# Decode heads turned back by transposes, the own key's value added on VectorE, and the two heads of a pair in turn

## What is computed

```python
h = rmsnorm(x, g_mix); proj = h @ w_in                 # pool channels | q | k | v, 512 columns each
x = x + concat(pool_mix(u), moba_attend(q, k, v)) @ w_out   # 8 heads of 64; decode: 256 cached keys + its own
x = x + cross_attend(rmsnorm(x, g_cross), mk, mv)      # 4 heads of 256, 256 memory keys for each sequence
x = x + square(relu(rmsnorm(x, g_mlp) @ w_up)) @ w_down
y = rmsnorm(x, g_final)
```

## Time and profile before

| | us |
|---|---|
| median of 3 runs | 451.04 |
| the three runs | 448.37, 451.04, 451.50 |
| profiled execution, first to last instruction (span) | 447.9 |
| TensorE busy | 423.8 |
| VectorE busy | 266.7 |
| ScalarE busy | 229.5 |
| GpSimd busy | 39.1 |

### The profile page before, as it was taken

The page is one execution under the profiler, slowest core; times in us unless marked ns, Lnnn a source line. Parts: engine busy times, 40 slices in busy tenths (PEclk is TensorE's granted clock), DMA queues, the critical chain, the costliest instruction groups (busy, mean ns, idle before and its releaser), DMA issues.

```text
span 447.9 us, 8424 instructions
## 1 busy us (share of the span) xinstructions
PE 423.8 (95%) x3346; PEld 393.0 (88%) x3346; DVE 266.7 (60%) x417; ACT 229.5 (51%) x411; POOL 39.1 (9%) x49
## 2 busy tenths in 40 slices
PE   2699899999999999999999999999999999999992
PEld 2699787787988999795599999999999999999992
DVE  2676787889454587654316967766666633444304
ACT  5777657664355474434026746656666533353202
POOL 0621001450000030000002200000000000020000
PEclk9979999999999999999989999999999999999998
DMA  7899897485699887597716655555555555545002
GB/s 273 286 280 343 324 265 240 161 283 170 185 352 317 334 277 284 173 368 281 266 36 246 235 190 187 189 190 189 187 187 184 186 180 176 176 168 179 1 1 97
DMA packets 42409, 96.80 MB, mean 216 GB/s; under 512 B 3954, under 2 KB 20466, under 8 KB 42234
## 3 DMA queue, kind: packets, MB, share of 16 engines
q1 hardware_dynamic: 40962, 93.03, 60.9%
q10 hardware_dynamic: 1408, 3.23, 1.9%
HBM read 91.94 MB, written 4.54 MB: 215 GB/s over the span
## 4 chain that ended last, share of the span: by engine, by line
PE 77%; ACT 8%; DVE 7%; issue 3%; DMA 2%; POOL 2%; ACTq 0%; SPq 0%; DVEq 0%; POOLq 0%
PE psum L865 68%; PE psum L666 4%; ACT w_hi L881 2%; DVE w_lo L1080 2%; DMA raw<-in_w_in 2%; POOL ssq L1306 1%; ACT swapped L881 1%; PE psum L791 1%; PE psum L778 1%; ACT soft L1024 1%; ACT act_hi L881 1%; DVE soft L1191 1%; PE psum L813 1%; DVE stats L1194 1%; PE psum L686 0%
## 5 line engine op out<-in xcount | busy, mean ns | idle before, releaser
L1080 DVE TENSOR_TENSOR w_lo<-raw,w_hi 128x1024 fp32r<-128x1024 f32 x82 | 103.1, 1268 | 90.5 <-ACT w_hi L881 90.0
L865 PE MATMUL psum<-act_hi,w_hi 128*128 128x264 f32 (+1 forms) x416 | 122.5, 294 | 9.0 <-DVE act_lo L1084 8.0
L881 ACT ACTIVATE w_hi<-raw 128x1024 fp32r<-128x1024 f32 x82 | 85.5, 1054 | 76.3 <-PE psum L865 64.2
L865 PE MATMUL psum<-act_lo,w_hi 128*128 128x264 f32 (+1 forms) x416 | 119.7, 288 | 0.0
L865 PE MATMUL psum<-act_hi,w_lo 128*128 128x264 f32 (+1 forms) x416 | 119.5, 287 | 0.0
L865 PEld LDWEIGHTS psum<-act_hi,w_hi 128*128 128x128 f32 x416 | 80.2, 193 | 12.9 <-DVE w_lo L1080 8.3
L865 PEld LDWEIGHTS psum<-act_lo,w_hi 128*128 128x128 f32 x416 | 80.0, 192 | 0.2
L865 PEld LDWEIGHTS psum<-act_hi,w_lo 128*128 128x128 f32 x416 | 79.8, 192 | 0.0
L1306 POOL TENSOR_TENSOR ssq<-ssq,sq 128x264 f32<-128x264 f32 (+1 forms) x31 | 25.4, 818 | 339.5 <-ACT sq L902 337.0
L865 PE MATMUL psum<-hid_hi,w_hi 128*128 128x264 f32 x176 | 50.1, 284 | 0.0
L865 PE MATMUL psum<-hid_lo,w_hi 128*128 128x264 f32 x176 | 50.1, 284 | 0.0
(11 more groups left out here) (155 smaller groups left out, 769.1 us busy)
## 6 DMA issues: line engine op xcount, KB each, us to landing
raw<-in_w_down SPq DMA_DIRECT2D x20, 512.0 KB, 3.3
raw<-in_w_up SPq DMA_DIRECT2D x18, 512.0 KB, 4.3
raw<-in_w_in SPq DMA_DIRECT2D x16, 512.0 KB, 5.4
raw_more<-in_w_up SPq DMA_DIRECT2D x14, 512.0 KB, 4.4
raw_more<-in_w_down SPq DMA_DIRECT2D x12, 512.0 KB, 4.2
keysT<-in_cache_k SPq DMA_DIRECT2D x16, 256.0 KB, 4.4
stage<-in_cache_v SPq DMA_DIRECT2D x16, 256.0 KB, 4.1
raw<-in_w_ck SPq DMA_DIRECT2D x8, 512.0 KB, 5.2
```

Source lines behind the costliest of these rows:

```text
L865: mm = pe.matmul(out, a, b, start=first and m == 0, stop=end_ and m == 2)
L881: return nc.scalar.activation(out, in_, ACT.Copy, scale=scale)
L1080: V.tensor_tensor(lo_of(c), raw_of(c), hi_of(c).bitcast(F32), ALU.subtract).then_inc(w_lo_ready, 1)
```

## The change

Five things are changed.

- `c_attn` and `xc_attn` transpose `opart` in full, 128x128 four times, and the copies out of PSUM pick each head's element with strides (`own_heads`). With that the tables `diag_q`, `diag_x`, `rowsel` and `own` go, and VectorE's pass into `opart` becomes a plain copy for `xc_O`.
- `xc_attn` is one job for each batch and half, four in all; the copies are in two parts for each (two rows of ScalarE and two of VectorE).
- The own key's weight is taken straight from the softmax (`ownp`, one column for each batch), and VectorE adds weight times `vown` to the result of `cO` as it writes `opart`. The product of line 743 and the one of line 737 go, and with the latter the wait for `t_copied`.
- `vown` holds the own value of each sample in its 32 rows. GpSimd loads it: once the three stores of `v_nat` have landed in HBM (`v_stored`), it issues 8 transfers that read back `v_sample`, one row each, spread over 32 partitions. They stand ahead of `add_squares("m")`.
- `S` and `O` issue the products of the two heads of a pair in turn; `S(2i)` and `S(2i+1)` both wait for their banks first.

```diff
-        ("xc_O", 1, 0), ("xc_attn", 0), ("xc_O", 1, 1), ("xc_attn", 1))
+        ("xc_O", 1, 0), ("xc_attn", 0, 0), ("xc_attn", 0, 1), ("xc_O", 1, 1), ("xc_attn", 1, 0), ("xc_attn", 1, 1))
...
+OPART_END = {("cO", b): ("c_attn", b) for b in range(2)} | {("xc_O", b, h): ("xc_attn", b, h) for b in range(2) for h in range(2)}
...
-        sb("beside_projections", [P, (3 * AT + 8) * T - KT * MEM - 2 * D], F32, mixers)
+        vown = sb("vown", [P, 2, AW], F32, mixers)
+        sb("beside_projections", [P, (3 * AT + 8) * T - KT * MEM - 2 * D - 2 * AW], F32, mixers)
         v_nat = sb("v_nat", [P, 3, AW], F32, mixers)
-        ownp = sb("ownp", [DEC, P], F32, mixers)
+        ownp = sb("ownp", [P, 2], F32, mixers)
...
+        def own_heads(job, part):
+
+            what, b, *half = job
+            t0 = SEQ + 4 * b
+            B = psum[:, PLACE[job][0], :]
+            out = []
+            for e in range(2):
+                if what == "c_attn":
+                    rows, k = slice(e * HD, (e + 1) * HD), slice(AT, KT)
+                    src = bass.AP(tensor=B.tensor, offset=B.offset + e * HD * 8 * CN + e, ap=[[8 * CN, HD], [P + 2, AT], [32, 4]])
+                else:
+                    rows, k = slice(0, P), slice(AT * half[0] + 2 * e, AT * half[0] + 2 * e + 2)
+                    src = bass.AP(tensor=B.tensor, offset=B.offset + 2 * e * P + 2 * half[0] + e, ap=[[8 * CN, P], [P, 2], [32, 4]])
+                out.append((part[rows, k, t0:t0 + 4], src, mix_hi[rows, k, t0:t0 + 4]))
+            return out
...
                 elif what == "S":
                     h = i[0]
+                    if h % 2:
+                        return
                     if h == 0:
                         pe.wait_ge(rope_done, 2 * AT)
-                    r, f = HD * (h % 2), h // 2
-                    q, k = qT[r:r + HD, f, :], kT[r:r + HD, f, :]
-                    pe.matmul(B[:, 0:P], q[:, 0:P], k[:, 0:P], start=True, stop=True)
-                    last = pe.matmul(B[:, P:3 * P], q[:, P:2 * P], k[:, 0:SEQ], start=True, stop=True)
+                    begin(("S", h + 1))
+                    pair = [(bank_of(("S", h + e)), qT[HD * e:HD * e + HD, h // 2, :], kT[HD * e:HD * e + HD, h // 2, :]) for e in range(2)]
+                    for S, q, k in pair:
+                        pe.matmul(S[:, 0:P], q[:, 0:P], k[:, 0:P], start=True, stop=True)
+                    for e, (S, q, k) in enumerate(pair):
+                        end(("S", h + e), pe.matmul(S[:, P:3 * P], q[:, P:2 * P], k[:, 0:SEQ], start=True, stop=True))
+                    return
...
                 elif what == "O":
                     for e in range(2):
-                        h = 2 * i[0] + e
-                        t = SOFT_T["P_T", h]
-                        wait_out(pe, ("P_T", h))
-                        if h == 0:
-                            for tt in range(3):
-                                wait_out(pe, ("v_nat", tt))
-                        o, pT = B[HD * e:HD * e + HD, :], softT[:, t % SOFT_TS, :]
-                        pe.matmul(o[:, 0:SEQ], v_nat[:, 0, h * HD:(h + 1) * HD], pT[:, 0:SEQ], start=True, stop=False, skip_group_check=True)
-                        last = pe.matmul(o[:, P:SEQ], v_nat[:, 1, h * HD:(h + 1) * HD], pT[:, SEQ:3 * P], start=False, stop=True, skip_group_check=True)
+                        wait_out(pe, ("P_T", 2 * i[0] + e))
+                    if i[0] == 0:
+                        for tt in range(3):
+                            wait_out(pe, ("v_nat", tt))
+                    for c in range(2):
+                        for e in range(2):
+                            h = 2 * i[0] + e
+                            o, pT = B[HD * e:HD * e + HD, :], softT[:, SOFT_T["P_T", h] % SOFT_TS, :]
+                            last = pe.matmul(o[:, c * P:SEQ], v_nat[:, c, h * HD:(h + 1) * HD], pT[:, c * SEQ:(c + 2) * P if c == 0 else 3 * P], start=c == 0, stop=c == 1, skip_group_check=True)
...
                     for c in range(2):
-                        pe.transpose(B[:, c * P:(c + 1) * P], p[:, c * P:(c + 1) * P], ident)
-
-                    last = pe.matmul(B[0:DEC, PAST:PAST + P], p[:, PAST:PAST + 1].broadcast_to([P, DEC]), ident, start=True, stop=True)
+                        last = pe.transpose(B[:, c * P:(c + 1) * P], p[:, c * P:(c + 1) * P], ident)
                 elif what == "cO":
                     b = i[0]
                     wait_out(pe, ("cP_T", b))
                     pT = softT[:, SOFT_T["cP_T", b] % SOFT_TS, :]
 
-                    pe.matmul(B, ownp[:, :], v_nat[0:DEC, 2, :], start=True, stop=False, skip_group_check=True)
                     for c in range(2):
                         for j in range(4):
                             if c == 0:
                                 landed(pe, ("V", 4 * b + j))
-                            last = tile4(B[32 * j:32 * j + 32, :], pT[:, c * P + 32 * j:c * P + 32 * j + 32], chunked(("V", 4 * b + j))[:, c, :], j, False, c == 1)
-                elif what == "c_attn":
-                    b = i[0]
-                    wait_out(pe, ("cO", b))
+                            last = tile4(B[32 * j:32 * j + 32, :], pT[:, c * P + 32 * j:c * P + 32 * j + 32], chunked(("V", 4 * b + j))[:, c, :], j, c == 0, c == 1)
+                elif what in ("c_attn", "xc_attn"):
+                    of = ("cO" if what == "c_attn" else "xc_O", *i)
+                    wait_out(pe, of)
                     for f in range(AT):
-                        last = pe.matmul(B[:, 4 * f:4 * f + 4], opart[:, OPART["cO", b] % 2, f * P:(f + 1) * P], con("rowsel"), start=True, stop=True)
+                        last = pe.transpose(B[:, f * P:(f + 1) * P], opart[:, OPART[of] % 2, f * P:(f + 1) * P], ident)
...
-                elif what == "xc_attn":
-                    b = i[0]
-                    for half in range(2):
-                        wait_out(pe, ("xc_O", b, half))
-                        for f in range(AT):
-                            last = pe.matmul(B[:, 4 * (AT * half + f):4 * (AT * half + f) + 4], opart[:, OPART["xc_O", b, half] % 2, f * P:(f + 1) * P], con("rowsel"), start=True, stop=True)
...
+                    copy(softT[:, n % SOFT_TS, 0:size], B[:, 0:size]).then_inc(free, 1)
+                elif what in ("c_attn", "xc_attn"):
+                    wait_full(act, job)
+                    for _, src, high in own_heads(job, mix_hi):
+                        last = copy(high, src)
+                    last.then_inc(hi_ready, 1)
...
-                parts = {"S": [(0, P), (P, 3 * P)], "cS": [(0, NKEY)]}.get(what, [(0, MEM), (MEM, 2 * MEM)])
+                if what == "cS":
+                    V.tensor_scalar(ownp[:, i[0]:i[0] + 1], soft[:, slot, PAST:NKEY], stats[:, slot, 4:5], None, ALU.mult).then_inc(own_weight_ready, 1)
+                parts = {"S": [(0, P), (P, 3 * P)], "cS": [(0, PAST)]}.get(what, [(0, MEM), (MEM, 2 * MEM)])
...
-                elif what == "cP_T":
-                    b = i[0]
-                    dve.wait_ge(t_copied, b + 1)
-                    if b:
-                        wait_full(dve, ("cO", b - 1))
-                    V.tensor_tensor(ownp[:, :], B[0:DEC, PAST:PAST + P], con("own", DEC)[:, b * P:(b + 1) * P], ALU.mult).then_inc(free, 1)
                 elif what in ("cO", "xc_O"):
                     wait_full(dve, job)
                     prior = before(OPART, job, 2)
                     if prior:
                         wait_full(dve, OPART_END[prior])
-                    diag = con("diag_q") if what == "cO" else con("diag_x")[:, 2 * i[1]:2 * i[1] + 2]
-                    heads = diag.shape[1]
-                    V.tensor_tensor(opart[:, OPART[job] % 2, :].rearrange("p (h n) -> p h n", h=heads), B.rearrange("p (h n) -> p h n", h=heads),
-                                    diag.unsqueeze(2).broadcast_to([P, heads, CN // heads]), ALU.mult).then_inc(free, 1)
-                elif what in ("O", "xP_O", "c_attn", "xc_attn", "pool"):
+                    if what == "cO":
+                        dve.wait_ge(vown_landed, 16 * DEC)
+                        dve.wait_ge(own_weight_ready, i[0] + 1)
+                        V.scalar_tensor_tensor(out=opart[:, OPART[job] % 2, :], in0=vown[:, i[0], :], scalar=ownp[:, i[0]:i[0] + 1], in1=B, op0=ALU.mult, op1=ALU.add).then_inc(free, 1)
+                    else:
+                        V.tensor_copy(opart[:, OPART[job] % 2, :], B).then_inc(free, 1)
+                elif what in ("c_attn", "xc_attn"):
+                    dve.wait_ge(hi_ready, HI[job] + 1)
+                    for dst, src, high in own_heads(job, mix_lo):
+                        last = V.tensor_tensor(dst, src, high.bitcast(F32), ALU.subtract)
+                    last.then_inc(free, 1)
...
+            gp.wait_ge(v_stored, 48)
+            gp.wait_ge(rope_done, 2 * AT)
+            v_rows = outs["v_sample"].rearrange("l b a h d -> (l b a) (h d)")
+            for s in range(DEC):
```

(18 more changed lines are left out.)

6 lines of the change are left out of this document (2 added, 4 removed).

## The result

| | median us | runs |
|---|---|---|
| kernel before | 449.83 | 17 |
| changed kernel | 446.27 | 17 |

The ratio is 0.9908, with a 95% interval of 0.9889 to 0.9927: the change makes the kernel 0.9% faster. Timed again beside other kernels it was 0.9933 (0.9906 to 0.9960). The profiled span went from 447.9 to 444.5, by 3.4 us.

What follows compares the result with a forecast made beforehand. TensorE, busy 95%, was taken as the bound, except about 47 to 102 us, where ScalarE and VectorE were. +3.3 - 1.43 - 0.3 = +1.6 us, span 449.5; with 3.1 carried over, 452.6; range 448.3 to 455.0.

Steps and rivals of the forecast that it cites:

- the issue time c: Time GpSimd needs to issue one of its eight transfers; taken as 1.0 us, with 0.53 as lower bound.
- the +3.3 at 102.47: Late transfers and a clock fall make TensorE ready only at 105.8, so work after VectorE's `mkT` comes 3.3 us later.
- The formula: Delay of ScalarE's square of tile 4: 73.3 + 8c + 0.78 - 79.09 us; 3.0 us at c = 1.0.
- A: Rival: the transfers fit in, c 0.63 or less, nothing late; -1.7 us, 449.3; chance 0.32.
- the decode products: `cO(1)` at 106.19 and `c_attn(1)`, in TensorE's stretch: dropped product -1.05, transposes -0.38, together -1.43 us.
- the tail: End of cross attention: the second `xc_attn`'s cheaper transposes gain 0.3 us, between 0 and 0.65.
- The terms hidden before 102.47: Savings in `cO(0)`, line 737 and `c_attn(0)`, 2.0 us: none reaches the end while VectorE's chain stands.
- D: Rival: the shorter tail keeps TensorE's clock at the end of cross attention, 1.6 us more gained, 447.7; chance 0.07.
- B: The forecast case: c from 0.75 to 1.2, transfers late; 450.6 to 454.2, likeliest 452.6; chance 0.42.
- C: Rival: GpSimd and VectorE hold each other up; with c = 1.5, `ck` 6.7 us late, 456.6; chance 0.14.
- The pairs' order: `S` and `O` issuing a pair's two heads in turn: taken as 0, bounded by 0.3 us either way.
- The wait for `vown`: In `cO(0)`: loads land before VectorE's reader; a wait there would tie VectorE to GpSimd and refute the prediction.

Runs made afterwards that it cites:

- 16 issues: Changed kernel with GpSimd's 8 transfers as 16 of half a row each, the same bytes: 450.53 us, ratio 1.0009.
- The padded table: Kernel before, table of cross attention's folds padded with zero columns from 4 to 64: 449.26 us, ratio 1.0000; run again 448.02, ratio 0.9984.
- the sums later: Changed kernel, GpSimd's first three additions ahead of its transfers and its pooling sums waiting until VectorE split 22 chunks: 446.07 us, ratio 0.9911.

## Why the prediction was wrong

**The step that failed is the issue time c.** The prediction had ScalarE's 0.53 as the lower bound and took 1.0, by the ratio of the engines' additions. Measured: 0.51 an issue, in both kernels, with 64 and with 32 KB. The nearest row, an issue on another engine, was right; the ratio came from arithmetic on 128x256 elements and said nothing about issuing. So the delay of 3.0 us at the square was 0.08, and the +3.3 at 102.47 did not come. The Trainium skill, "DMA: Bandwidth & Descriptors", section "Latency and other measured facts", gives about 1 us to the first byte of a software-generated transfer. No run here shows a first byte; 2.9 to 5.8 us passed from issue to landing, and the engine was held for 0.51.

The formula stood: 74.20 + 4.10 + 0.78 - 79.09 is 0.0. But its start of 73.3 was 0.9 early (74.20; 72.57 to 75.49 in all eight profiles with the loads), and with 74.20 the bound below which nothing is late is c = 0.51 instead of 0.63. The transfers fitted in with nothing to spare. With 16 issues the formula gives 72.57 + 8.11 + 0.78 = 81.46, and the square stood at 81.54; `ck` came 2.6 later than before and the work at 102.47 3.7, where the forecast for 3.0 us of delay had 2.7 and 3.3.

**A and its sum.** With c right, A is what remains: -1.43 for the decode products, -0.3 for the tail. Measured -1.50 and -0.20 between the first two profiles; 1.4 for the first stands in seven of eight profiles, the second is within their spread. The terms hidden before 102.47 stayed hidden: TensorE's wait grew from 0.57 to 1.88. The 0.36 gained at 102.47 in the first profile lies ahead of `ck` and is not the change's: the second profile of the changed kernel is there 1.35 us later than the first.

**A missed the median too, by 3.0 us.** Its 449.3 lacks the 1.5 of the clock at the end of cross attention. And 1.3 of it is the 3.1 us carried over from span to median. In every execution of which time and span are both known the time is 1.7 to 2.0 us above the span, 1.8 on average. The profiled one of the kernel before, of 447.9, then took about 449.7; the prediction compared it with the median of three others. The span by A and D together, 447.9 - 1.7 - 1.6 = 444.6, meets the measured 444.5 closely, with some luck in the terms that cancel.

**The clock (D) came, for another reason.** The prediction tied it to a shorter tail and gave it 0.07. The tail still has its waits (0.31 and 0.81). The padded table shows what went with it: the same matmuls, the same 2.0 us, the same wait, and no fall. What differs is what TensorE streamed before the fall, 4 columns or 64 in each of the 16 products. Where it streamed 4, the granted clock went to half (1.2 GHz) once or twice between 218 and 232 us in four profiles of four; with 64 or 128, in none of ten.

**The clock behind `ck`.** The prediction had it fall there in B and C and not in A. A holds, and it fell in five profiles of seven: the 1.05 us saved in `cO(0)` and what else goes there lengthen the wait without `ck` being late. At 102 us nothing of it is left: in the first profile TensorE waits 0.6 us for `mix_lo` and 0.3 for `mkT` on the way there, in the second for neither. It fits this that the mean granted clock of the changed kernel's executions (0.9868 and 0.9843) is no higher than that of the kernel before (0.9877 on the chip of the second), though the fall at the end of cross attention is gone.

**The pairs' order** was rightly taken as 0. **C** did not occur: the issues were 0.498 us at the median beside VectorE's passes, and no slower. That GpSimd and VectorE hold each other up is seen only where both compute (the splits at 2.82).

**The wait for `vown`.** The prediction put the landing of the loads ahead of `cO(0)`'s reader and named a wait there as a sign against it. It was close. The last load was issued at 77.80 and took 5.8 us to land, to 83.60; the reader started at 83.79, right behind `uext`. The margin was 0.2 us. With the sums later the last issue is at 79.1, its landing took up to 6.4, and the reader started 0.2 later behind `uext` than in the changed kernel.

**What stays open.** The spans account for 3.4 us, the medians for 3.6, the first ratio for 4.1 and the second for 3.0; runs of one kernel spread over 3 to 8 us. The padding took the fall away in the profiles of the kernel before, but only 0 to 0.16% off its time. Part of the gap is seen in the two profiles: from the second chunk of `co` to the end they take 218.15 and 218.17 us where the kernel before takes 217.80, and 0.1 more from `P_T(6)` to the first fold. Why is not shown, and the rest is open. By the transposes alone, on the kernel before, the time went down by 0.34% (0.04 to 0.65).

## What to carry to other kernels

A cost that no row shows is first taken from the nearest instruction of its own kind, here another engine's issue of a transfer; a ratio between engines' arithmetic is not a ratio of their issues. Where a row of TensorE's small products streams only a few columns, look at the granted clock of the next chunk: widening them to 64 columns cost 0.05 us and took away, in three profiles of three, a fall that cost 1.5. In the medians this shows in one of the two kernels only, so it has to be timed in each. And price the products that go by where they stand: of 5.5 us of TensorE's work, about 1.6 reached the end, and the part saved ahead of a wait for VectorE brought a new fall of the clock, which the waits behind it happened to absorb. A span and a median of other executions are not to be mixed: the offset was 3.1 us in the forecast and 1.8 within one execution.

## What the runs showed of the hardware

- An issue of a transfer on GpSimd's queue held it for 0.51 us on average, at 64 KB and at 32 KB, with the first of a row at 0.66; ScalarE's store of `v_sample` was 0.53.
- 60 of the 64 columns that the padded folds stream are zero, and the granted clock from 218 to 231 us was 1.00 in three profiles, where it was 0.81 to 0.87 in four with the 4 columns alone.
- TensorE's wait ahead of `ck` was 1.78 to 2.28 us in seven profiles, and the granted clock fell to half behind it in five; behind waits of 0.57 to 0.60 at the same place it fell in none of six.
- At the low clock, products of 264 columns are 0.22 us apart instead of 0.12.
- A strided pick of 128x8 elements from PSUM took 0.17 us on ScalarE and 0.16 on VectorE; a dense one of 128x32 took 0.20 on ScalarE and 0.18 to 0.19 on VectorE before. With sizes this different no price of the strides can be read from them, only that it is small.
